# A third seven-product group per quarter, and turns of the MLP's hidden tile in quadrants through HBM

## The reference

```
h2 = rms_norm(x, norm_ffn_g)
u = square(relu(h2 @ w_up))        # w_up 2048 x 8192
x = x + u @ w_down                 # w_down 8192 x 2048
return rms_norm(x, norm_final_g)
```

## Time and profile before

| | |
|---|---|
| median of the runs | 1476.49 us |
| the profiled execution's own time | 1476.18 us |
| its span, first to last instruction | 1474.4 us |
| matmuls | 6968 |
| granted TensorE clock | 0.999 |
| bytes by DMA | 299.33 MB, 60% of the DMA engines' time |

### The profile page before, as it was taken

The page is one execution under the profiler, slowest core; times in us unless marked ns, Lnnn a source line. Parts: engine busy times, 40 slices in busy tenths (PEclk is TensorE's granted clock), DMA queues, the critical chain, the costliest instruction groups (busy, mean ns, idle before and its releaser), DMA issues.

```text
span 1474.4 us, 18772 instructions
## 1 busy us (share of the span) xinstructions
PE 1465.7 (99%) x6968; PEld 1279.8 (87%) x6968; DVE 1190.9 (81%) x1558; ACT 766.8 (52%) x986; POOL 15.0 (1%) x21
## 2 busy tenths in 40 slices
PE   9999999999999999999999999999999999999997
PEld 8888888888888888888888888888888888888886
DVE  7977887776577788777799988888897888889877
ACT  7656565444455555444445555555554555555553
POOL 0000000000000000000000000000000000000000
PEclk9999999999999999999999999999999999999999
DMA  9556544667655566556765665656666656655563
GB/s 333 191 169 211 184 154 164 229 203 241 213 180 184 186 199 206 194 200 200 248 233 181 202 219 201 218 185 207 217 204 202 208 199 226 214 199 193 198 209 114
DMA packets 149801, 299.33 MB, mean 203 GB/s; under 512 B 5232, under 2 KB 5360, under 8 KB 149488
## 3 DMA queue, kind: packets, MB, share of 16 engines
q1 hardware_dynamic: 149168, 297.51, 59.9%
q10 hardware_dynamic: 576, 1.06, 0.2%
HBM read 296.45 MB, written 2.10 MB: 202 GB/s over the span
## 4 chain that ended last, share of the span: by engine, by line
PE 98%; issue 1%; DVE 1%; POOLq 0%; POOL 0%; DVEq 0%; ACT 0%
PE acc L545 88%; PE acc L827 3%; PE banks L776 3%; PE acc L776 1%; PE banks L564 1%; PE banks L583 1%; PE banks L573 0%; PE banks L591 0%; DVE ta_lo L1775 0%; PE banks L680 0%; PE banks L696 0%; PE banks L695 0%; PE banks L693 0%; PE acc L603 0%; DVE final L1787 0%
## 5 line engine op out<-in xcount | busy, mean ns | idle before, releaser
L865 ACT ACTIVATE whi<-raw 128x1024 fp32r<-128x1024 f32 x542 | 569.2, 1056 | 577.3 <-PE acc L545 517.9
L1222 DVE TENSOR_TENSOR wlo<-raw,whi 128x1024 fp32r<-128x1024 f32 x542 | 655.1, 1223 | 213.1 <-ACT whi L865 208.5
L545 PE MATMUL acc<-whi,ta_hi 128*128 128x512 f32 x1308 | 497.4, 380 | 0.0
L545 PE MATMUL acc<-wlo,ta_hi 128*128 128x512 f32 x1308 | 495.7, 379 | 0.0
L545 PE MATMUL acc<-whi,ta_lo 128*128 128x512 f32 x1308 | 495.7, 379 | 0.0
L545 PEld LDWEIGHTS acc<-whi,ta_hi 128*128 128x128 f32 x1308 | 247.2, 189 | 36.7 <-issue 1.2
L545 PEld LDWEIGHTS acc<-whi,ta_lo 128*128 128x128 f32 x1308 | 247.2, 189 | 35.1
L545 PEld LDWEIGHTS acc<-wlo,ta_hi 128*128 128x128 f32 x1308 | 247.3, 189 | 34.5
L545 PE MATMUL acc<-whi,tb_hi 128*128 128x512 f32 x560 | 212.3, 379 | 0.0
L545 PE MATMUL acc<-wlo,tb_hi 128*128 128x512 f32 x560 | 212.2, 379 | 0.0
L545 PE MATMUL acc<-whi,tb_lo 128*128 128x512 f32 x560 | 212.2, 379 | 0.0
(11 more groups left out here) (208 smaller groups left out, 1049.2 us busy)
## 6 DMA issues: line engine op xcount, KB each, us to landing
raw<-in_w_in SPq DMA_DIRECT2D x64, 1024.0 KB, 5.2
raw<-in_w_up SPq DMA_DIRECT2D x64, 1024.0 KB, 5.3
raw<-in_w_down SPq DMA_DIRECT2D x57, 1024.0 KB, 5.0
raw<-in_w_gate SPq DMA_DIRECT2D x32, 1024.0 KB, 5.3
raw<-in_w_att SPq DMA_DIRECT2D x16, 1024.0 KB, 5.0
raw<-in_w_ret SPq DMA_DIRECT2D x16, 1024.0 KB, 5.0
raw<-in_w_out SPq DMA_DIRECT2D x16, 1024.0 KB, 5.0
raw<-in_w_down SPq DMA_DIRECT2D x14, 512.0 KB, 4.3
```

Source lines behind the costliest of these rows:

```text
L545: last = nc.tensor.matmul(paired(acc[B.parity][:, t, :]), a[:, k, tok], halves_in_turn(b), start=(k == 0 and n == 0), stop=(k == (B.ends + ...
L865: nc.scalar.activation(whi[:, B.ring_at(u), :], raw[:, B.raw_at(u), :], ACT.Copy).then_inc(hi_ready, 1)
L1222: V_.tensor_tensor(wlo[:, at, :], raw[:, B.raw_at(u), :], whi[:, at, :].bitcast(f32), ALU.subtract).then_inc(lo_ready, 1)
```

## The change

**What it does.** A quarter is described by a new class `Quarter`. `LATE` names two late groups: in up block 0 for hidden group 3 as before, and in up block 2 for hidden group 2 of the quarter before, both for columns 0 and 1. The first two down blocks of quarters 0 to 2 have therefore 4 units each and not 6. The last quarter keeps its number of products.

```diff
-TOP = KCH - 2 * UCH
 SUMS, MIXED, PRODUCTS = 3, 4, 3
-FOLDS = (5, 7)
+BOUNDARY_FOLDS, LATE_FOLDS = 5, 7
+BOUNDARY = (2, 3, 3)
+LATE = {0:(0,1,3),2:(0,1,2)}
...
+            if hosted:
+                n = list(LATE).index(i)
+                mixed = (q - 1) * MIXES_OF_QUARTER + (1 if LATE[i][2] == GROUPS - 1 else 2)
+                self.late[i] = Group(E, UNITS - 2, q * GROUPS_OF_QUARTER - (len(LATE) - n),
+                                     q * FOLDS_OF_QUARTER - LATE_FOLDS * (len(LATE) - n), mixed, LATE[i], False)
+                before += 2 * UCH
+            self.up.append((E, Block(B6 + i, 8, q, before)))
...
+            self.down = [Block(D0, 8, q, 0, self.units[0] - 1), Block(D1, 8, q, -left_out[0], self.units[1] - 1)]
...
+        parking = nc.dram_tensor("parking", (GROUPS, P, TILES * COLS), f32, kind="Internal").ap()
+        in_quads = buf[3][:].rearrange("p t (o n) -> p (t o) n", n=S)
+        exchanged_at = buf[1][:].rearrange("p t (i n) -> p (t i) n", n=S).rearrange("p i (a n) -> p i a n", n=SQ)
```

SP:

```diff
+            def load_up(Q, q, i):
+                (E, tail), G = Q.up[i], Q.late[i]
+                col = q * D + i * COLS
+                load_rows(E, w_up, col, 0, range(3))
+                if G:
+                    load_left(G, q * D - D)
+                    load_right(G, q * D - D)
+                load_rows(tail, w_up, col, 0, range(3, 4))
...
+                if last:
+                    if AGAIN:
+                        sp.wait_ge(folded, q * FOLDS_OF_QUARTER)
+                    sp.dma_start(gfin[:], g_fin.partition_broadcast(P)).then_inc(fin_full, 16)
```

TensorE:

```diff
+                    else:
+                        gemm(E, ta_hi, ta_lo, 0, 6)
+                        if G:
+                            seven_products(G)
+                        gemm(tail, ta_hi, ta_lo, 6, 8)
+                pe.wait_ge(t_free, q * 4 + (T_STAGE6 + 2))
+                gemm(Q.down[0], tb_hi, tb_lo, 0, 4)
...
+                        gemm(Q.down[0], tb_hi, tb_lo, 4, Q.units[0])
+                    gemm(Q.down[1], tb_hi, tb_lo, 0, Q.units[1])
+                    if Q.units[2] > 4:
+                        pe.wait_ge(t_free, q * 4 + (T_STAGE6 + 3))
+                gemm(Q.J, tb_hi, tb_lo, 0, Q.units[2])
```

ScalarE:

```diff
+                Q = Quarter(q, first, last)
+                if AGAIN and not first:
+                    act.wait_ge(mixed_set, ((q - 1) * MIXES_OF_QUARTER + 1) * MIXED)
+                    fetch(2, Q.turn(q, 0))
+                for i in range(1 if first else 0, GROUPS):
+                    (E, tail), G = Q.up[i], Q.late[i]
+                    split(E, 0, 2)
+                    if i > 1:
+                        hi_from_exchanged(Q.turn(q, i - 1), i - 2)
+                    split(E, 2, 4)
...
+                        squared_relu(Q.up[i - 1][1])
+                    if AGAIN and not first and i == 1:
+                        mixed_hi_of(GROUPS - 2, (q - 1) * MIXES_OF_QUARTER + 1)
+                    if G:
+                        split_for_seven(G, E, 4, parks=(q * 4 + i, i - 1) if i else None)
+                        split(tail, 6, 7)
...
+                        split(E, 4, 5)
+                        if i:
+                            park(q * 4 + i, i - 1)
+                        split(E, 5, 7)
+                    if i:
+                        fetch_next(Q, q, i, first)
+                    split(tail, 7, 8)
...
+                    split(Q.down[1], 0, 1)
+                    park(q * 4 + 4, 3)
+                    split(Q.down[1], 1, 2)
+                fetch_next(Q, q, 4, first)
...
+                    split(Q.down[1], 2, 4)
+                    split(Q.J, 0, 1)
+                    hi_from_exchanged(Q.turn(q, 4), 3)
+                    split(Q.J, 1, 2)
+                    mixed_hi_of(GROUPS - 1, q * MIXES_OF_QUARTER)
...
+            def park(n, g):
+                act.wait_ge(quads_turned, n)
+                act.dma_start(parking[g], in_quads.rearrange("p o n -> p (o n)")).then_inc(parked, 16)
...
+            def fetch(g, n):
+                for o in range(QUADS):
+                    act.dma_start(exchanged_at[o * SQ:(o + 1) * SQ].rearrange("f i a n -> f i (a n)"),
+                                  parking[g].rearrange("(i f) (o n) -> o f i n", f=SQ, o=QUADS)[o]).then_inc(exchanged, 16)
+            def fetch_next(Q, q, i, first):
+                act.wait_ge(parked, (q * 4 + i) * 16)
...
+                fetch(i - 1, Q.turn(q, i))
...
+            def split_for_seven(G, B, begin, squares_of=None, parks=None):
+                u = G.at
+                split(B, begin, u - 1)
+                if parks:
+                    park(*parks)
                 if squares_of:
...
+                sums_hi(G, 0, 1)
+                sums_hi(G, 1, 2)
+                split(B, u - 1, u)
+                sums_hi(G, 2, 3)
+                split(B, u, u + 3)
```

VectorE (the folds are in the order of before):

```diff
+                    else:
+                        split(E, 0, 2)
+                        if i == 1 and AGAIN and not first:
+                            mixed_tokens(Q.turn(q, 0), (q - 1) * MIXES_OF_QUARTER + 1)
+                        if i > 1:
+                            lo_from_exchanged(q * 4 + (12 + i - 1), i - 2)
+                        split(E, 2, 4)
+                        turn_in_quads(q * 4 + i)
+                        if i == 1 and AGAIN and not first:
...
+                    if G:
+                        if i:
+                            dve.wait_ge(quads_turned, q * 4 + i)
+                        sums_for_seven(G, (q - 1) * MIXES_OF_QUARTER + (2 if AGAIN and i else 1))
+                        fold_in_passing(G, tail)
+                        split(tail, 7, 8)
...
+                split(Q.down[0], 0, 2)
+                lo_from_exchanged(q * 4 + 15, 2)
+                split(Q.down[0], 2, 4)
+                turn_in_quads(q * 4 + 4)
...
+                split(Q.down[1], 0, 3)
+                if not last:
+                    add_residual(Q.down_end[0], 0)
+                split(Q.down[1], 3, 4)
+                if not wide:
+                    split(Q.J, 0, 1)
+                mixed_tokens(Q.turn(q, 4), q * MIXES_OF_QUARTER)
+                lo_from_exchanged(q * 4 + 16, 3)
+                if wide:
+                    split(Q.down[1], 4, 5)
+                else:
+                    split(Q.J, 1, 2)
+                mixed_lo_of(GROUPS - 1, q * MIXES_OF_QUARTER)
...
+            def turn_in_quads(n):
+                dve.wait_ge(u_ready, n)
+                if later(n - 1):
+                    dve.wait_ge(parked, (n - 1) * 16)
+                for o in range(QUADS):
+                    piece = V_.transpose(in_quads[:, o, :].rearrange("p (m t n) -> p m t n", t=TILES, n=SQ),
+                                         by_chunk(buf[0][:])[:, :, :, o * SQ:(o + 1) * SQ])
+                piece.then_inc(quads_turned, 1)
...
+            def sums_for_seven(G, mixes):
+                E, u = G.entries, G.at
+                left_up, left_low, right_low, right_up = corners(G)
+                T1, T2, T3 = weight_sums(G)
+                dve.wait_ge(raw_full[E.slot(u)], E.filled(u))
+                dve.wait_ge(corner_full, G.n * 16 + 16)
+                V_.tensor_tensor(T1, left_up, right_up, ALU.add).then_inc(sum_set, 1)
+                dve.wait_ge(raw_full[E.slot(u + 2)], E.filled(u + 2))
+                dve.wait_ge(sum_set, G.sums(1))
+                V_.tensor_tensor(T2, T1, right_low, ALU.add).then_inc(sum_set, 1)
+                split(E, u - 2, u - 1)
+                dve.wait_ge(mixed_lo_ready, mixes)
+                V_.tensor_tensor(T3, right_up, right_low, ALU.add).then_inc(sum_set, 1)
                 sums_lo(G, 0)
-                fourth_sum(G)
-                split(B, 5, 6)
+                dve.wait_ge(sum_set, G.sums(3))
+                V_.tensor_tensor(right_up, T2, left_low, ALU.add).then_inc(sum_set, 1)
+                split(E, u - 1, u)
                 sums_lo(G, 1)
-                split(B, 6, 8)
+                split(E, u, u + 2)
```

More of the change, by code:

```diff
@@ L479, in load_rows, with load_left, load_right @@
                     load(B, w[ds(row + s * 512, 512), ds(col, COLS)], s)
[L481 to L485 removed]
+            def load_left(G, row):
+                load(G.entries, w_down[ds(row + G.c * 512, 512), ds(G.j * COLS, COLS)], G.at // 2)
+            def load_right(G, row):
+                E, u = G.entries, G.at + 2
+                parts = [w_down[ds(row + k * P, UCH * P), ds(G.k * COLS, COLS)].rearrange("(k p) n -> p k n", p=P)
+                         for k in (G.lower.start, G.upper.start)]
                 for src in parts:
@@ L781, in seven_products @@
             def seven_products(G, J=None, K=None):
-                E, u = G.entries, UNITS - 2
+                E, u = G.entries, G.at
+                upper, lower = G.upper, G.lower
+                mixed_hi, mixed_lo = mixed_halves(G.c)
                 def units(k, t):
@@ L832, in rest @@
             def rest(B):
-                for u in range(2, UNITS):
```

(32 more changed lines are left out.)

392 lines of the change are left out of this document (205 added, 187 removed).

## The result

The changed kernel takes 1487.01 us (median of 4 runs, 1486.73 to 1488.99) against 1476.55 us for the kernel before on the same chip: ratio 1.0074, 95% interval 1.0061 to 1.0086. It is 10.5 us slower, where I had forecast 1.5; the time lies above my range (1472.3 to 1482.0). The profiled execution took 1488.99 us, 12.8 above the profiled one of before, so sums made from its trace come out about 2 us above what the typical run shows.

What follows compares the result with a forecast made beforehand. TensorE's matmul count was taken as the bound: profiled 1476.18 - 3.89 (matmuls) + 4.8 (block 2) + 0.6 (boundaries) = 1477.7, with 0.31 from profiled to median 1478.0 us; range 1472.3 to 1482.0.

Steps and rivals of the forecast that it cites:

- TensorE's matmuls set the end, so each lateness counts in full: Whole kernel: TensorE holds 98% of the chain, so anything delivered later than it wants adds to the end in full.
- Eighteen matmuls, 3.89 us: Up block 2, quarters 1 to 3: eight products become seven, six matmuls fewer each, saving 3.89 us.
- Transposes at the lower bound: Turns on VectorE: four 128x256 transposes taken at the time of 32x256 ones, 1.79 us a turn instead of 7.2.
- Block 2: T1 at 5.2, 1.6 us a group: Up block 2: first weight sum T1 starts 5.2 us in, after the turn; first fold late, 1.6 us three times, 4.8.
- The late group in up block 0, the three groups of the last quarter's end and its closing part keep their order, so I price them at nothing.: Up block 0 and the last quarter's end: order unchanged, so no added time, 0 us.
- The boundaries of quarters 0 to 2, 0.2 us each: From first down block to J's group: the fold ends at 18.3, wanted at 18.13; 0.2 us three times, 0.6 in all.
- T1 = R - 4.96: Boundaries of quarters 0 to 2: start of the group's first weight sum, counted from J's start; 3.8 us, now 2.4.
- R: Last turn of quarters 0 to 2: when ScalarE goes on after the store, 8.7 us into the first down block.
- The store's 3.5 us: Last turn of quarters 0 to 2: the 512 KB store lands in 3.5 us, being alone; bounds 3.0 and 6.8.
- the store holds ScalarE longer: Rival at the boundaries: store lands in 4.3 us, R is 9.5, each boundary costs 1.0; 1480.4 us, chance 0.26.
- the matmuls alone decide: Rival: VectorE's block 2 list is 1.6 us shorter than counted, both stalls vanish; 1472.6 us, chance 0.20.
- gfin, the splits in the up blocks, DMA traffic: gfin's later load, ScalarE's weight splits behind the store wait, and 18 MB more traffic: all covered, priced at nothing.

Runs made afterwards that it cites:

- The experiment on the last quarter's order: Changed kernel with VectorE splitting J's unit 0 before the waiting residual addition, ScalarE J's units 0 and 1 before the squares: 1482.63 us, 1.0045.
- the nine kernels: The changed kernel (1487.01 us) and the eight other kernels with both late groups and ScalarE's issues.
- GpSimd's own in the experiment: Changed kernel with every turn's store and loads issued by GpSimd, so that ScalarE waits for neither: 1502.63 us, 1.017 to the kernel before.
- the orders mended: Changed kernel with last quarter's order, corner earlier, deadline order except in block 0's group, and closing block's residual addition behind unit 4: 1476.99 us, 1.0003.

## Why the prediction was wrong, step by step

- *TensorE's matmuls set the end, so each lateness counts in full.* Right: matmul count and gaps give 11.9 of the 12.8 us, the kernel's start and end 0.7 more.
- *Eighteen matmuls, 3.89 us.* Right; the page has 6950.
- *Transposes at the lower bound.* Right: 64 of them at a median of 403 ns, four in 1.43 us, where I had 1.79.
- *Block 2: T1 at 5.2, 1.6 us a group.* Right: in quarter 2 unit 5 was wanted at 1187.16, so the block began at 1174.2 and T1 at 1179.50 stood at 5.3; gaps 1.6 to 1.8. In part this is luck: the turn was 0.36 us shorter than I took it, but began 0.24 later, and 0.24 us of hand-over before T1 was not in my sum. Block 0's group did not stall.
- *"The late group in up block 0, the three groups of the last quarter's end and its closing part keep their order, so I price them at nothing."* The first failed step, 4.6 us. I read the groups' own lists and not what stands ahead of T1: the first down block's last two units now run behind the second's first six, and its residual addition moved in front of J's units and so of the corner loads. The experiment on the last quarter's order took just this away and gained 4.4 us.
- *The boundaries of quarters 0 to 2, 0.2 us each.* The second failed step, 5.9 us in the profiled execution and 4.4 without its late turn, for 0.6. My T1 = R - 4.96 lacks a condition: T1 also needs SP's corner loads, which are released by VectorE's low half of J's unit 1, 5.2 to 5.5 us before T1 starts. I gave this no term; it held T1 for 0.98, 0.64 and 0.77 us. R was mis-sized besides, 9.0, 8.9 and 10.3 us for 8.7. The store's 3.5 us were too few (4.0, 3.7 and 4.1), because my reason, that it is alone, did not hold. The 10.3 contain 0.9 us from the turn before, which I had priced at nothing; that turn was late in this one execution. A last step of 0.2 to 0.3 us between R and VectorE's list is the rest.
- *The rival "the store holds ScalarE longer".* In direction it was the better case, but it did not come as described: its 4.3 us were reached by none of the last turns' stores (3.6 to 4.1 us in the nine kernels), and it knows nothing of the corner. Its 1480.4 us with the last quarter's 4.6 on top would make 1485.0. The fit of the Trainium skill ("DMA: Bandwidth & Descriptors", section "Anatomy of one DMA"), from which I had an estimated 3.2 us for the store, is given there for DMAs that GpSimd issues, and ScalarE issued these. The stores at the boundaries took 3.7 to 4.1 us, and GpSimd's own in the experiment 3.5 to 3.6, so all lie above that estimate.
- *The two steps together.* 4.6 us for the last quarter, 3.8 for the boundaries (4.4 for 0.6), 0.3 for block 2 and 0.2 of small gaps are 8.9 of the 9.0 us between forecast and measurement.
- *The rival "the matmuls alone decide".* It did not happen as built. With the orders mended it comes within 4.6 us of gaps, about what the eighteen matmuls give back.
- *gfin, the splits in the up blocks, DMA traffic.* At nothing, rightly as to gfin and the splits: gfin landed at 1461.7 and its reader came at 1469.6, and no gap stands in an up block outside the groups. The traffic was not free at the boundaries, where stores and corner loads are waited for.

What stays open: whether any order of VectorE's list in block 2 is free of gaps. T1 can't start before 5.3 us there by the turn's end, since the sums use the buffer that the turn reads, and there was no room for a second one, so this was not tried.

## What to carry to other kernels

VectorE is busy for 77 to 81% of the span, and yet it has no pause in the 14 us from T1 to the first fold, and there it is the bound. So price each step by its place in the in-order list against the next deadline behind it, not by the engine's spare time. Follow the start of every late chain back over all queues, the DMA that another engine's step releases too, and read the first instruction ahead of a part that "keeps its order". When a wait is removed, look one, two and three deadlines further before counting the gain: four of my experiments moved a wait instead of removing it.

## What was unexpected of the hardware

- A stalled matmul costs 0.16 us more than its bracket and makes the next 0.10 us late: 12.0 us of listed waits in 14 entries are 15.6 us of gaps. The 0.16 us lie in how the bracket is counted: it begins at the end of the matmul before, 0.38 us after its start, while at full pace the next one starts after 0.2159.
- The same kind of transfer lands after very different times beside the weight loads: the 16 stores of 512 KB took 3.7 to 7.8 us (median 4.4), the 76 loads of 128 KB 2.7 to 8.1 (median 4.8).
- With GpSimd issuing, a wait of 2.57 us at 1256.37 was followed by the lower of TensorE's two clocks (1.2 GHz for 2.4) and matmuls 0.43 us apart from 1257.6 to 1261.0, some 1.7 us more. No wait of the changed kernel, the longest 1.7 us, did that. Busy time in windows of that kernel, the granted clock third from the end:

```profile
1256.00:1258.00 2.00, 1.63 (x7) 1.40 (x8) 2.00 (x3) 2.00 (x3) 1.91 (x4) 0.89 0.34 96
1258.00:1261.00 3.00, 3.00 (x9) 2.37 (x8) 2.86 (x3) 0.31 (x1) 0.00 (x0) 0.51 1.01 288
1261.00:1264.00 3.00, 3.00 (x16) 2.62 (x15) 0.00 (x0) 0.00 (x0) 0.00 (x0) 1.00 1.05 259
```
